# Stick-breaking attention: the differences of the running products on GpSimd in place of VectorE

## The reference

```
z = (q @ k.T) * scale                                  # per head, 128 queries against keys 0..q1
strict = key position < query position
log_keep = where(strict, log_sigmoid(-z), 0)
log_rest = reverse_cumsum(log_keep) - log_keep
a = where(strict, exp(log_sigmoid(z) + log_rest), 0)
out = a @ v
```

## Time and profile before

| | |
|---|---|
| runs | 3102.27 us median of 3 (3101.62 to 3105.03) |
| profiled execution | 3100.76 us, span of its instructions 3098.6 us |
| busy in the span | PE 2978.1 us (96%), DVE 1505.4 (49%), ACT 724.1 (23%), POOL 390.4 (13%) |
| mean granted TensorE clock | 0.994 of full speed |
| stick-breaking units | DVE 356.8 to 397 us in the first layer, 886 to 926 us in the second |

### The profile page before, as it was taken

How to read it: one execution, slowest core, us unless ns; L and a number is a source line. 1 busy time by engine, 2 the same in 40 slices (tenths; PEclk the granted TensorE clock), 3 DMA queues, 4 the chain that set the end, 5 groups by cost and what they waited for, 6 DMA issues and landing times.

```text
span 3098.6 us, 36760 instructions
## 1 busy us (share of the span) xinstructions
PE 2978.1 (96%) x14781; PEld 1672.5 (54%) x14781; DVE 1505.4 (49%) x2837; ACT 724.1 (23%) x1524; POOL 390.4 (13%) x274
## 2 busy tenths in 40 slices
PE   8999899999989999999999999999999988999998
PEld 5888544788844444557657433333346545444443
DVE  5994862898394255886666211211155743111212
ACT  1211541131163211121124100110025642111111
POOL 3544000555300010020001000000000000000000
PEclk9999999999999999999999999999999999999999
DMA  5452002357200312202313999999921005999997
GB/s 227 154 215 84 28 1 109 147 190 275 81 12 14 134 58 85 108 34 70 143 55 128 409 382 391 390 380 374 388 81 66 1 3 206 421 421 420 421 421 294
DMA packets 89895, 605.86 MB, mean 196 GB/s; under 512 B 10806, under 2 KB 11607, under 8 KB 19328
## 3 DMA queue, kind: packets, MB, share of 16 engines
q1 hardware_dynamic: 79776, 575.70, 46.5%
q0 software_dynamic: 4432, 15.73, 1.7%
q10 hardware_dynamic: 5520, 12.09, 1.2%
HBM read 592.47 MB, written 11.01 MB: 195 GB/s over the span
## 4 chain that ended last, share of the span: by engine, by line
PE 62%; DVE 8%; ACT 2%; issue 1%; DVEq 0%; ACTq 0%
PE ps L2966 7%; PE ps L2928 7%; PE ps L1605 5%; PE ps L2979 4%; PE ps L2945 4%; PE ps L3009 4%; PE ps L1122 3%; PE ps L1406 3%; PE ps L3259 2%; PE ps L2816 2%; PE ps L3018 2%; PE ps L2833 2%; PE ps L1895 2%; PE ps L2730 2%; PE ps L3422 1%; PE ps L1520 1%
## 5 line engine op out<-in xcount | busy, mean ns | idle before, releaser
L637 PE MATMUL ps<-mem 128*128 128x256 f32 x1792 | 394.9, 382 | 10.3 <-DVE mem L667 9.4
L637 PEld LDWEIGHTS ps<-mem 128*128 128x128 f32 x1792 | 341.6, 191 | 62.8 <-DVE mem L667 12.9
L582 POOL TENSOR_TENSOR mem<-mem 128x512 f32<-128x512 f32 (+1 forms) x160 | 300.0, 1875 | 530.7 <-DVE mem L878 272.4
L780 DVE SCALAR_TENSOR_TENSOR mem<-mem 128x1024 f32<-128x1024 f32 x160 | 255.5, 1637 | 13.5 <-DMA mem<-in_ada_w 12.8
L2966 PE MATMUL ps<-mem 128*64 128x512 f32 x1024 | 223.3, 594 | 0.0
L2928 PE MATMUL ps<-mem 128*64 128x512 f32 x1024 | 222.5, 592 | 0.7 <-ACT mem L2862 0.7
L667 DVE TENSOR_TENSOR mem<-ps,mem 128x256 f32<-128x256 f32 x308 | 121.4, 419 | 111.9 <-PE ps L637 68.5
L1122 PE MATMUL ps<-mem 128*128 128x512 f32 x384 | 169.6, 597 | 1.8 <-DVEq L169 1.8
L1605 PE MATMUL ps<-mem 128*128 128x512 f32 x384 | 167.0, 594 | 0.2 <-ACT mem L1235 0.2
L3118 DVE TENSOR_TENSOR mem<-ps,mem 128x512 f32<-128x512 f32 x16 | 11.1, 692 | 313.7 <-PE ps L2928 313.7
L2966 PEld LDWEIGHTS ps<-mem 128*64 128x64 f32 x1024 | 72.1, 137 | 150.6 <-issue 150.6
(11 more groups left out here) (440 smaller groups left out, 4399.0 us busy)
## 6 DMA issues: line engine op xcount, KB each, us to landing
mem<-in_moe_w SPq DMA_DIRECT2D x384, 1024.0 KB, 14.1
mem<-in_w_in SPq DMA_DIRECT2D x48, 1024.0 KB, 7.3
mem<-in_ada_w SPq DMA_DIRECT2D x48, 1024.0 KB, 5.0
mem<-in_hy_w_in SPq DMA_DIRECT2D x24, 1024.0 KB, 6.9
mem<-in_w_out SPq DMA_DIRECT2D x12, 1024.0 KB, 5.9
mem<-in_k_win_l SPq DMA_DIRECT2D x8, 1024.0 KB, 7.4
mem<-in_hy_w_out SPq DMA_DIRECT2D x8, 1024.0 KB, 4.9
mem<-in_sw_w_in SPq DMA_DIRECT2D x6, 1024.0 KB, 7.0
```

The source lines that it names most:

```text
L582: gp(out, x, y, op).then_inc(A.mark(sem), 1)
L637: m = mm(seven(l, unit), x[:, k, :], y[:, k, :], start=(k == 0), stop=(k == 3))
L780: stt(PRODUCT if again else w, w, 1.0, C_ROWS[:, z, :], ALU.mult, ALU.mult, accum_out=mod(layer, b // KD, b % KD, z))\
```

## The change

The subtraction of line 1086 leaves DVE's list. A new function on GpSimd, `pool_attn`, does the same subtraction on the same buffers for the 16 stick-breaking units of each layer. DVE marks `g_ready` after the second scan, GpSimd waits for that and marks `f_ready`, and PE's transposes of a stick-breaking unit wait for `f_ready` in place of `weights`. The counts of `weights` for the forgetting units go down by the 16 units that no longer mark it. Nothing else moves.

```diff
+        FIRST_STICK = 4 * NQ
+
+        def pool_attn(A):
+            A.last, A.counts = None, {}
+            for n in range(4 * NQ):
+                u = FIRST_STICK + n
+                kw = (UN[u][2] + 1) * P
+                pset = P_SETS[u % 4]
+                A.e.wait_ge(S["g_ready"], n + 1)
+                nc.gpsimd.tensor_tensor(pset[:, :, 512 - kw:512], pset[:, :, 513 - kw:513], pset[:, :, 512 - kw:512],
+                                        ALU.subtract).then_inc(A.mark("f_ready"), 1)
+            A.e.wait_ge(*A.last)
...
-                    A.e.wait_ge(S["weights"], u + 1)
+                    if kind == 1:
+                        A.e.wait_ge(S["f_ready"], u - FIRST_STICK + 1)
+                    else:
+                        A.e.wait_ge(S["weights"], u + 1 if kind == 0 else u - FIRST_STICK + 1)
...
-                                .then_inc(A.mark(), 1)
-                        A.e.wait_ge(*A.last)
-                        tt(pset[:, :, 512 - kw:512], pset[:, :, 513 - kw:513], pset[:, :, 512 - kw:512], ALU.subtract)\
-                            .then_inc(A.mark("weights"), 1)
+                                .then_inc(A.mark("g_ready" if c else None), 1)
...
+                if p in (2, 2 + H_PHASES):
+                    pool_attn(A)
```

## The result

The changed kernel takes 3113.78 us in the median of 6 runs (3106.17 to 3117.18), the kernel before 3101.99 in 6 runs beside them (3101.62 to 3105.28): slower by 11.8 us in the medians. The forecast was 3115. The total came out, but its parts did not: the rounds cost only a quarter of what the sum gave them, and the rest was lost in places that the prediction called unchanged.

A forecast was written before the change was run, and what follows sets the result against it. DVE was taken to bound the attention stage: 9.83 - 3.42 + 4.80 + 0.10 + 0.30 = 11.6 us a round, 7.1 a layer less 0.6, 13.0 in all; from 3102.27 to 3115.3, said as 3115, range 3104 to 3124.

The forecast's parts named there:

- the sum: Stick-breaking attention: DVE's round 11.6 us, 1.78 over 9.83; with 0.6 off per layer, 6.5 a layer, 13.0 in all.
- Removed: 3.42: DVE's round: four differences (2.96 us) and their waits for the scans (0.46) go, leaving 6.41 of 9.83.
- The scan is held, once, between the next unit's two scans: DVE's scans: GpSimd's subtraction stops DVE between the next unit's two scans, 2.08 ns a column.
- The first rival: DVE's scans are not held, PE takes the path: 3092, or 3098 with half the gain or less left; chance 0.13.
- the second: DVE and GpSimd don't alternate; holds and scans stand one after the other: round 12.9, total 3127 us; chance 0.08.
- Three holds, 4.80 us: DVE's round: holds by the 512, 768 and 1024 units' subtractions add 1.06 + 1.60 + 2.14 us.
- The late sigmoid, 0.30: DVE's round: a new wait for the 768 unit's sigmoid, some 0.6 us, mostly under the 512 unit's hold; 0.3 added.
- DVE is full, so its busy time sets the round: Attention stage: DVE busy 39.18 of 40.00 us, so each microsecond per round on DVE counts on the end, 8 times.
- The end of the stage, 0.6 back: After each layer's last scan: DVE's 0.60 us maximum from PSUM isn't stopped by the last hold, so 0.6 comes off.
- The units before and after unchanged: Listed among the signs for the changed kernel's profile: units before and after keep their times; no cost was given them.
- a sign of being wrong: PE's granted clock in the attention stage falling from 1.00 with longer idle times; not in the forecast total.

The follow-up runs named there:

- e5: Changed kernel with each subtraction replaced by two GpSimd fills of the same buffer, which write without reading SBUF: 3107.41 us, +5.5 (1.0016).
- e8: Kernel before plus nine forms of a GpSimd operation on 1024 columns, each twice, in the first layer's output phase: 3106.25 us in one run.
- e9: Kernel before plus 17 idle GpSimd instructions (16 fills and a wait) in the first layer's output phase: 3106.91 us, +3.7 (1.0013).
- e11: Kernel before with only the 256-column units' differences on GpSimd, plus 123 idle GpSimd instructions in the first layer's output phase: 3099.43 us, -3.75 (0.9991).
- e4: The changed kernel run once more, unaltered, for a second profile: 3111.87 us, +10.1 over the kernel before (1.0031).
- e10: Changed kernel plus 111 idle GpSimd instructions (110 fills and a wait) in the first layer's output phase: 3107.65 us, +4.5 over the kernel before (1.0013).
- e6: Kernel before with only the 256-column units' differences moved to GpSimd, VectorE making all others: 3104.56 us, +2.7 (1.0007).

## Why the prediction was right in its total and wrong in its parts

**Removed: 3.42.** Right within 0.2. The plain work that DVE keeps is 0.58 (copy) + 1.27 (512 scans) + 4.74 (six scans, e5, start to start) = 6.59, against 6.41.

**The scan is held, once, between the next unit's two scans.** Right: 2.04 against 0.41 us, 7.60 against 4.83 for six, and GpSimd waits in turn (2.29 for 768 columns at 372.16, more than the 1.92 of 1024). The first rival falls with it (and e5 shows that it was priced too well: without holds the round is 9.07, 0.8 under before, where it allowed 1.2). So does the second: the scans never stand for two subtractions, and the round did not pass 12.5.

**Three holds, 4.80 us: the term that failed.** Measured: two holds, 7.52 - 4.74 = 2.78. The lengths were taken from additions of two buffers, while these subtractions read one buffer twice; e8 prices that at 1.89 for 2.35, a fifth less. (Line 882 in the earlier trace rows is a product and not an addition; nothing rests on it.) And the third hold, the 512 unit's, adds next to nothing to the wait for the sigmoid (next point).

**The late sigmoid, 0.30.** With the 512 unit's hold the sum gave this place 1.06 + 0.30 = 1.36; measured, it is one idle stretch of 0.91. The sum let GpSimd start 0.3 after DVE falls idle, which no row had shown; it starts 0.09 after (369.29 to 369.38), so that its 1.04 are over 0.2 after the sigmoid is there.

**DVE is full, so its busy time sets the round.** Wrong in the changed kernel, and this is the step that the sum is built on. DVE's parts do add up afterwards, 6.59 + 0.91 + 2.78 = 10.3, but the 0.91 is whatever is left until the sigmoid. The round is the loop over the 1024 unit's subtraction, PE, ACT and the scans of 768 and 1024, and of the holds only the 1.2 on the 1024 unit's scan lengthens it, as e5 shows. The prediction saw the loop, but charged it as a 0.3 on top of every hold. At 1.5 us a layer the kernel would have been 3 us slower, inside what can't be told from no change.

**The end of the stage, 0.6 back.** Not seen there: the last two ways from copy to copy are 0.33 and 0.28 longer. What comes back, 0.45, lies ahead of the first copy.

**The units before and after unchanged.** Wrong, and worth more than the change itself: PE waits about 4 us more for line 667 in the second layer's projections because 17 instructions stand ahead of a pause of GpSimd, shown by adding and taking away idle instructions (e9 to e11). The prediction asked only what is queued behind the subtractions in their own phase. No row quoted ahead of it priced this, though the gap of 0.43 stood in the trace. And the clock fell: for 3.6 us' worth in the two phases, to a mean of 0.92 in the second layer's stage (894 to 938 us), which the prediction had named as a sign of being wrong, and for about 1.9 between them.

So 13.0 was predicted and 11.8 came, with 10 too much in the rounds and 9 not foreseen elsewhere: that the total was right is chance.

**What stays open.** Whether the half clock belongs to the change. Its phases had one or two such stretches each in e4 and e10, but those of the kernel before had none in one profile and two, back to back, in the second layer of e9 and of e8, whose attention is before's. One profile a kernel cannot settle it. Nor was it tried why GpSimd pauses where it does, 128 instructions apart: in the long kernels no such gap shows at these additions, and in e6, where 5 instructions stand ahead, it shows nowhere in the second layer's projections. Which of its readings makes a two-buffer form slower is open too. And 1.9 to 3.6 us of the changed kernel's 10.1 to 11.8 are in neither of the two parts that were run alone (8.2), which is no more than the noise of the three.

## What to carry to other kernels

Price an instruction moved to GpSimd by a row with the same layout of inputs, not by one with the same number of columns, and charge a hold only where it lies on the loop that sets the round: one that falls beside a wait which the engine has anyway costs nothing. Instructions added to one engine also move everything behind them along that engine's own count: compare a stretch that the diff doesn't touch in both traces before believing a small total, and see whether idle instructions alone do the same.

## What the runs showed of the hardware

In the projections GpSimd paused 0.26 us more than usual at its instructions 196 and 324 (before), and at 324 and 452 once 128 more stood ahead (e10, e11); with 17 ahead (e9) the gap was gone there and the kernel 3.7 us slower in the median (interval 1.2 to 6.8). GpSimd took 1.89, 2.35 or 2.68 us for the same 1024 columns by the layout of its inputs. Two fills of 768 columns (0.74 each) ran across a unit's scans of 512 without holding them (e5: 4.83 for six scans, 7.60 beside the subtractions).
